# DeltaNet mixer on one Trainium2 core: read-out normed and projected by token block, one weight split moved, one barrier replaced by flags

## The reference, cut to what matters

```python
q, k, v = jnp.split(silu(conv(proj[..., :3*kd])), 3, axis=-1)   # l2norm on q and k
o = gated_delta_rule_chunked(q, k, v, beta, g)                  # chunks of 64 tokens
o = o * lax.rsqrt(jnp.mean(o * o, axis=-1, keepdims=True) + RMS_EPS) * norm_g
o = o * jax.nn.silu(z).reshape(b, s, DN_HEADS, DN_HEAD_DIM)
return h + o.reshape(b, s, kd) @ w_out
```

## Time and profile before

| what | value |
|---|---|
| median of 3 runs | 2733.64 us (2732.69 to 2733.97) |
| the profiled execution | 2735.75 us |
| its span, first to last instruction | 2733.7 us |
| TensorE busy | 2642.7 us, 97% of the span |
| VectorE, ScalarE, GpSimd busy | 2015.5, 1472.7, 86.8 us |
| mean granted TensorE clock | 0.988 of full |

### The profile page before, as it was taken

One profiled execution on the slowest core, in us unless ns is written; L12 is line 12 of the kernel. 1 busy time (PEld: TensorE's weight loads), 2 busy tenths in 40 slices (PEclk: granted clock), 3 DMA queues, 4 the chain that ended last, 5 costly groups with the idle time before them and its releaser, 6 DMA issues.

```text
span 2733.7 us, 46442 instructions
## 1 busy us (share of the span) xinstructions
PE 2642.7 (97%) x18206; PEld 2254.9 (82%) x18206; DVE 2015.5 (74%) x1904; ACT 1472.7 (54%) x1446; POOL 86.8 (3%) x82
## 2 busy tenths in 40 slices
PE   8999999999999989999999898999999999999998
PEld 7889887888889888888889887787787878787776
DVE  6666876666666956676667755888888888888787
ACT  5443514444444514455446624676777677776765
POOL 6000006000000000000000000000000000000000
PEclk9999999999999999999999998999999999999999
DMA  8564313555563305555564405999999999999893
GB/s 275 192 191 154 114 49 124 191 192 171 195 193 129 109 18 170 193 187 170 194 189 139 140 3 200 348 342 348 340 337 349 345 339 347 346 340 346 317 351 119
DMA packets 342896, 601.48 MB, mean 220 GB/s; under 512 B 11984, under 2 KB 180816, under 8 KB 342608
## 3 DMA queue, kind: packets, MB, share of 16 engines
q1 hardware_dynamic: 335264, 590.85, 62.6%
q10 hardware_dynamic: 7472, 8.32, 0.9%
HBM read 598.08 MB, written 1.05 MB: 219 GB/s over the span
## 4 chain that ended last, share of the span: by engine, by line
PE 62%; DMA 22%; DVE 8%; ACT 3%; DVEq 2%; issue 1%; another core or an unknown queue 1%; ACTq 0%; PEldq 0%; SPq 0%; PEld 0%; POOLq 0%
PE ps L2856 13%; PE ps L565 8%; DMA raw<-in_ffn_w_down 8%; PE ps L589 7%; PE ps L2885 7%; PE ps L2860 6%; DMA raw<-in_w_in 6%; PE ps L568 4%; DVE wlo L314 4%; DMA raw<-in_dn_w_in 4%; PE ps L2890 3%; DMA work<-in_moe_w_gate 2%; ACT whi L310 2%; DVEq L316 1%; DMA raw<-in_ffn_w_up 1%
## 5 line engine op out<-in xcount | busy, mean ns | idle before, releaser
L314 DVE TENSOR_TENSOR wlo<-raw,whi 128x2048 fp32r<-128x2048 f32 (+1 forms) x394 | 903.2, 2292 | 217.5 <-ACT whi L310 209.2
L310 ACT CAST whi<-raw 128x2048 fp32r<-128x2048 f32 (+1 forms) x394 | 751.3, 1908 | 402.0 <-DMA raw<-in_ffn_w_down 142.7
L2856 PE MATMUL ps<-whi,xboth 128*128 128x512 f32 x1792 | 459.4, 398 | 6.1 <-issue 2.3
L565 PE MATMUL ps<-xboth,whi 128*128 128x512 f32 x1680 | 420.8, 392 | 0.0
L2856 PEld LDWEIGHTS ps<-whi,xboth 128*128 128x128 f32 x1792 | 330.1, 188 | 81.7 <-issue 15.2
L565 PEld LDWEIGHTS ps<-xboth,whi 128*128 128x128 f32 x1680 | 305.3, 189 | 57.2
L314 DVE TENSOR_TENSOR wlo<-U,whi 128x2048 fp32r<-128x2048 f32 x112 | 256.4, 2289 | 53.4 <-ACT whi L310 50.5
L310 ACT CAST whi<-U 128x2048 fp32r<-128x2048 f32 x112 | 214.2, 1912 | 82.2 <-DMA U<-in_moe_w_up 73.7
L568 PEld LDWEIGHTS ps<-xboth,wlo 128*128 128x128 f32 x1680 | 229.2, 190 | 16.4
L2860 PE MATMUL ps<-wlo,xboth 128*128 128x512 f32 x896 | 240.1, 390 | 0.5 <-DVE wlo L314 0.5
L568 PE MATMUL ps<-xboth,wlo 128*128 128x256 f32 x1680 | 234.2, 282 | 0.0
(11 more groups left out here) (538 smaller groups left out, 3624.7 us busy)
## 6 DMA issues: line engine op xcount, KB each, us to landing
raw<-in_moe_w_gate SPq DMA_DIRECT2D x58, 1024.0 KB, 5.8
raw<-in_moe_w_up SPq DMA_DIRECT2D x56, 1024.0 KB, 6.0
U<-in_moe_w_up SPq DMA_DIRECT2D x56, 1024.0 KB, 5.8
U<-in_moe_w_down SPq DMA_DIRECT2D x56, 1024.0 KB, 5.6
raw<-in_ffn_w_gate SPq DMA_DIRECT2D x55, 1024.0 KB, 5.2
raw<-in_ffn_w_up SPq DMA_DIRECT2D x55, 1024.0 KB, 5.3
raw<-in_ffn_w_down SPq DMA_DIRECT2D x55, 1024.0 KB, 4.8
work<-in_moe_w_gate SPq DMA_DIRECT2D x54, 1024.0 KB, 6.0
```

Of the source, the lines that this page charges most:

```text
L310: act.copy(whi[:, n % SPLIT, 0:width], buf[:, 0:width]).then_inc(hi_ready[n % RAW], 1)
L314: dve.tensor_tensor(wlo[:, n % SPLIT, 0:width], buf[:, 0:width], whi[:, n % SPLIT, 0:width], ALU.subtract).then_inc(split_ready[n % SPLIT], 1)
L565: pe.matmul(ps[:, first_bank + b, :], whi[:, n % SPLIT, c * GW + b * P:c * GW + (b + 1) * P], xboth[:, c].rearrange("p a t -> p (a t)"), s ...
L2856: pe.matmul(dst, part[:, k * C // 2 + c, xhalf(q)], whi[:, (m + k) % SPLIT, c * EW:(c + 1) * EW], start=(k == 0 and c == 0 and part is xhi ...
```

## The change

The last step of dn_in no longer splits a tile; dn_core begins with that split on ScalarE and VectorE. dn_core is taken out of `APART`. TensorE transposes block 0 of the read-out (`dn_turn_out_tensor`) between the two halves of block 1's read-out, and block 1 after the first two weight tiles of the projection. ScalarE and VectorE carry out norm, gate and the split into `xhi` and `xlo` for block 0 and then for block 1, with a flag per part (`dn_lo`) for TensorE. The normed read-out lies in the place of `dn_qe`, since `work[:, 0:2048]` still holds `dn_R`. The projection (`dn_project_tensor`) runs tiles 0 to 2 for block 0, tiles 0 to 2 for block 1, then tile 3 for both; a tile's slot is given back after block 1. ScalarE issues a square root of a constant ahead of its Squares. ScalarE's and VectorE's parts of dn_out stay as they are.

```diff
@@ -171,13 +171,13 @@
-APART = ("rwkv", "dn_in", "dn_core")
+APART = ("rwkv", "dn_in")
@@ -2064,7 +2064,7 @@
 ...
         dn_decayed = state_in(work[:, 9216:10240])
-        dn_sq, dn_on = dn_W, th_in(work[:, 0:2048])
+        dn_sq, dn_on = dn_W, dn_qe
         dn_out = work[:, 2048:4096].rearrange("p (h t) -> p h t", h=NH)
@@ -2249,7 +2249,8 @@
 ...
                 tap.then_inc(f["dn_tap"], 1)
-                split_hi(act, m + SPLIT)
+                if j < DN_TILES - 1:
+                    split_hi(act, m + SPLIT)
                 if 1 <= j <= DN_CONV:
@@ -2324,8 +2325,9 @@
 ...
                     tap.then_inc(f["dn_conv"], 1)
-                take(dve, hi_ready[(m + SPLIT) % RAW])
-                split_lo(dve, m + SPLIT)
+                if j < DN_TILES - 1:
+                    take(dve, hi_ready[(m + SPLIT) % RAW])
+                    split_lo(dve, m + SPLIT)
             return n + DN_TILES
@@ -2337,7 +2339,7 @@
 ...
-        def dn_core_tensor(pe):
+        def dn_core_tensor(pe, n, l):
             for t in range(TT):
@@ -2381,9 +2383,6 @@
 ...
             r0, r1 = HALVES
-            def quarter(first, h):
-                return ps[:, first + h // 4, (h % 4) * P:(h % 4 + 1) * P]
@@ -2436,12 +2435,54 @@
 ...
             dn_out_tensor(pe, 1, 2)
-            for t in range(TT):
-                pe.wait_ge(f["dn_on"], t + 1)
-                for h in range(NH):
-                    tr = pe.transpose(ps[:, (6, 0)[t] + h // 4, (h % 4) * P:(h % 4 + 1) * P], dn_on[:, t, h, :],
-                                      const("ident"))
-                tr.then_inc(f["dn_oT"], 1)
+            return n
+        def dn_turn_out_tensor(pe, t):
+            pe.wait_ge(f["dn_on"], t + 1)
+            if t:
+                pe.wait_ge(f["dn_om2"], 2 * t)
+            for h in range(NH):
+                tr = pe.transpose(quarter(6, h), dn_on[:, t, h, :], const("ident"))
+            tr.then_inc(f["dn_oT"], 1)
+        DN_OUT_TILES = C // 2
+        EARLY_TILES = DN_OUT_TILES - 1
+        def dn_project_part(pe, n, j, t):
+            pe.wait_ge(f["dn_lo"], 2 * t + j // 2 + 1)
+            last = j == DN_OUT_TILES - 1
+            blocks = [(b, s) for b in range(2) for s in range(2)]
+            if last:
+                blocks = [(b, s) for s in range(2) for b in range(2)]
+            for b, s in blocks:
+                for k, (wp, part) in enumerate(PASSES):
+                    mm = pe.matmul(ps[:, 2 * t + s, :], (xhi, xlo)[part][:, 2 * j + b, t * P:(t + 1) * P],
+                                   wp[:, (n + j) % SPLIT, b * D + s * HALF:b * D + (s + 1) * HALF],
+                                   start=(j == 0 and b == 0 and k == 0), stop=(last and b == 1 and k == 2),
+                                   skip_group_check=True)
+                if last and b == 1:
+                    mm.then_inc(f["y_part"], 1)
+            if t == TT - 1:
+                mm.then_inc(tile_done[(n + j) % SPLIT], 1) if not last else pe.drain().then_inc(tile_done[(n + j) % SPLIT], 1)
+        def dn_project_tensor(pe, n, l):
+            for j in range(EARLY_TILES):
+                take_split(pe, n + j)
+                dn_project_part(pe, n, j, 0)
+                if j == 1:
+                    dn_turn_out_tensor(pe, 1)
+            for j in range(EARLY_TILES):
+                dn_project_part(pe, n, j, 1)
+            take_split(pe, n + EARLY_TILES)
+            for t in range(TT):
+                dn_project_part(pe, n, EARLY_TILES, t)
+            return n + DN_OUT_TILES
+        def quarter(first, h):
+            return ps[:, first + h // 4, (h % 4) * P:(h % 4 + 1) * P]
@@ -2456,6 +2497,7 @@
 ...
             if t == 1:
+                dn_turn_out_tensor(pe, 0)
                 pe.wait_ge(f["dn_ss"], 3)
@@ -2466,7 +2508,9 @@
 ...
-        def dn_core_scalar(act):
+        def dn_core_scalar(act, n, l):
+            split_hi(act, n - 1 + SPLIT)
@@ -2490,20 +2534,22 @@
 ...
                 act.copy(dn_A[:, c - 1], wide_two((6, 0)[c - 1])).then_inc(f["dn_as"], 1)
+            act.activation(tiny[:, 72:73], small("one"), ACT.Sqrt)
             for t in range(TT):
 ...
                 act.activation(dn_sq[:, t], wide_two((4, 2)[t]), ACT.Square).then_inc(f["dn_sqd"], 1)
-            act.wait_ge(f["dn_om"], 2)
-            act.activation(dn_ms, dn_tmp, ACT.Sqrt, bias=small("eps"), scale=1.0 / P).then_inc(f["dn_or"], 1)
-            for t in range(TT):
+                act.wait_ge(f["dn_om"], t + 1)
+                act.activation(dn_ms[:, t], dn_tmp[:, t], ACT.Sqrt, bias=small("eps"), scale=1.0 / P).then_inc(f["dn_or"], 1)
                 for q in range(2):
 ...
                              dn_out[:, 4 * q:4 * q + 4, t * P:(t + 1) * P]).then_inc(f["dn_hi"], 1)
-        def dn_core_vector(dve):
+            return n
+        def dn_core_vector(dve, n, l):
             d_ = dve.drain
+            take(dve, hi_ready[(n - 1 + SPLIT) % RAW])
+            split_lo(dve, n - 1 + SPLIT)
             for t in range(TT):
@@ -2537,35 +2583,40 @@
 ...
                     dve.tensor_copy(dn_R[:, 2], bank(2)).then_inc(f["dn_rs"], 1)
+                    dn_unit_vector(dve, 0)
                 d_()
 ...
                 dve.tensor_tensor(dn_S[c], dn_decayed, wide_two((6, 0)[c - 1]), ALU.add).then_inc(f["dn_ss"], 1)
-            for t in range(TT):
-                dve.wait_ge(f["dn_sqd"], t + 1)
-                dve.tensor_reduce(dn_tmp[:, t], dn_sq[:, t], AX.X, ALU.add)
-                d_()
-                dve.tensor_tensor(dn_tmp[:, t], dn_tmp[:, t], dn_rqq[:, t], ALU.mult).then_inc(f["dn_om"], 1)
-            dve.wait_ge(f["dn_or"], 1)
-            dve.reciprocal(dn_ms, dn_ms)
+            dn_parts_vector(dve, 0)
+            dn_unit_vector(dve, 1)
+            dn_parts_vector(dve, 1)
+            return n
+        def dn_unit_vector(dve, t):
+            d_ = dve.drain
+            dve.wait_ge(f["dn_sqd"], t + 1)
+            dve.tensor_reduce(dn_tmp[:, t], dn_sq[:, t], AX.X, ALU.add)
             d_()
-            dve.tensor_tensor(dn_ms, dn_ms, dn_rq, ALU.mult)
+            dve.tensor_tensor(dn_tmp[:, t], dn_tmp[:, t], dn_rqq[:, t], ALU.mult).then_inc(f["dn_om"], 1)
+            dve.wait_ge(f["dn_or"], t + 1)
+            dve.reciprocal(dn_ms[:, t], dn_ms[:, t])
             d_()
-            for t in range(TT):
-                dve.tensor_tensor(dn_on[:, t], wide_two((4, 2)[t]), per_token(dn_ms, t), ALU.mult).then_inc(f["dn_on"], 1)
-            for t in range(TT):
-                dve.wait_ge(f["dn_oT"], t + 1)
-                tk = slice(t * P, (t + 1) * P)
-                for q in range(2):
-                    dve.scalar_tensor_tensor(out=dn_out[:, 4 * q:4 * q + 4, tk], in0=wide_one((6, 0)[t] + q),
-                                             scalar=second_vec("dn_norm_g_2")(0),
-                                             in1=U[:, DN_Z + 4 * q:DN_Z + 4 * q + 4, tk], op0=ALU.mult,
-                                             op1=ALU.mult).then_inc(f["dn_om2"], 1)
-            for t in range(TT):
-                tk = slice(t * P, (t + 1) * P)
-                for q in range(2):
-                    dve.wait_ge(f["dn_hi"], 2 * t + q + 1)
-                    dve.tensor_tensor(xlo[:, 4 * q:4 * q + 4, tk], dn_out[:, 4 * q:4 * q + 4, tk],
-                                      xhi[:, 4 * q:4 * q + 4, tk], ALU.subtract)
+            dve.tensor_tensor(dn_ms[:, t], dn_ms[:, t], dn_rq[:, t], ALU.mult)
+            d_()
+            dve.tensor_tensor(dn_on[:, t], wide_two((4, 2)[t]), per_token(dn_ms, t), ALU.mult).then_inc(f["dn_on"], 1)
+        def dn_parts_vector(dve, t):
+            tk = slice(t * P, (t + 1) * P)
+            dve.wait_ge(f["dn_oT"], t + 1)
+            for q in range(2):
+                dve.scalar_tensor_tensor(out=dn_out[:, 4 * q:4 * q + 4, tk], in0=wide_one(6 + q),
+                                         scalar=second_vec("dn_norm_g_2")(0),
+                                         in1=U[:, DN_Z + 4 * q:DN_Z + 4 * q + 4, tk], op0=ALU.mult,
+                                         op1=ALU.mult).then_inc(f["dn_om2"], 1)
+            for q in range(2):
+                dve.wait_ge(f["dn_hi"], 2 * t + q + 1)
+                dve.tensor_tensor(xlo[:, 4 * q:4 * q + 4, tk], dn_out[:, 4 * q:4 * q + 4, tk],
+                                  xhi[:, 4 * q:4 * q + 4, tk], ALU.subtract).then_inc(f["dn_lo"], 1)
@@ -3239,22 +3290,13 @@
 ...
+        STREAM["dn_core"] = lambda sp, n, l: n
+        TENSOR["dn_core"], VECTOR["dn_core"], SCALAR["dn_core"] = dn_core_tensor, dn_core_vector, dn_core_scalar
+        TENSOR["dn_out"] = dn_project_tensor
```

(15 more changed lines are left out.)

## The result

Four runs of the changed kernel took 2713.44 to 2716.94 us, median **2715.79**; four of the kernel before 2732.69 to 2736.09, median 2733.80. The ratio is 0.9932 [0.9920, 0.9943]: 18.0 us less. The forecast was 2717.2, 16.4 less, in a range of 2714 to 2723. The profiled execution took 2713.44 us, its span is 2711.5, against 2735.75 and 2733.7. It is the fastest of its four, so the two profiles lie further apart than the medians.

The account below looks back on a forecast made before the run. TensorE, with 62% of the span in the chain of waits, was taken to bound the kernel. The moved split's -3.4 and the tail's -13.0 make -16.4 us: 2717.2 on the median 2733.64, range 2714 to 2723.

Parts of the forecast that it names:

- The tail, -13.0: From the read-out's old end to the last projection matmul, TensorE takes 24.1 us in place of 37.1.
- The slacks: In the projection, inputs ready before TensorE asks: 0.9 us at second transposes, 0.3 at block 1's tiles, 0.5 at fourth tile.
- rival (a): In the projection, the new waits come late and become holes, with the clock possibly falling: 2721 us; chance 0.10.
- The moved table load: ScalarE's 1.28 us load for the square root, moved ahead of block 0's Square into an idle stretch: worth nothing.
- The moved split, -3.4: At dn_core's start, TensorE begins earlier and VectorE's second product starts at 1556.88 in place of 1560.25: 3.4 us less.
- everything in the solve follows: In dn_core, all of the solve was to shift with VectorE's second product, by 3.4 us (3.2 with the low clock).
- -4.0, if TensorE alone led: The split term's upper bound in dn_core: 4.0 us less if TensorE, not VectorE, led.
- Rival (b): The moved split sits on dn_core's path, so the first term is 0: 2720.6 us; chance 0.06.
- Route and experts unchanged: The stages behind the projection follow unchanged, so the -13.0 us is kept and the first expert tile comes 16 us earlier.
- (c): The weight copies pace the experts, so that stage starts only 11.0 us earlier: 2722.6 us; chance 0.03.
- (d): Slower than before: copies' lead over the first expert tile shrinks by 5.4 us, experts lose 30 us: 2747; chance 0.03.
- Code placement a microsecond either way: For the total, where the code falls was to spread the forecast by a microsecond either way.

Follow-up runs that it names:

- e3: Changed kernel with the barrier, the old projection by weight tile and the last split in dn_in kept, so only the norm goes by block: 2736.90 us.
- e5: Changed kernel with the projection in the old order, weight tile by weight tile for both token blocks, block 1's transposes ahead of it: 2723.22 us.
- e6: Kernel before with 15 dummy matmuls behind dn_in's last matmul, ahead of the barrier, and TensorE's wait for VectorE's decays ahead of them: 2731.14 us.
- e1: Kernel before with only the last weight split moved from dn_in to the start of dn_core; barriers, norm and projection as they were: 2731.48 us.
- e2: Kernel before with 20 and 17 dummy matmuls on zeros (the fillers) in TensorE's two holes at the end of dn_core: 2740.62 us.
- e8: Changed kernel with 37 tiny matmuls on zeros, without use, in TensorE's hole in the route stage: 2723.04 us.
- e9: Changed kernel with 15 dummy matmuls in the route stage and VectorE's two memsets moved to where it waits for the ranks: 2715.39 us.
- e11: Kernel before, unchanged, profiled once more: 2733.91 us.

## Why the prediction was right

*The tail, -13.0*: measured -13.2; the run that has the tail without the moved split has the same piece, and gains 13.9 us with the route's 1.7 in it. Its parts held too. The first hole is 0.33 us (forecast 0.5); the matmuls took 5.76 + 16.34 = 22.1 (21.8); the two batches of transposes 1.02 and 0.87 (0.9 each). The slacks were enough: block 1 was scaled at 1629.98, 1.2 us before TensorE turned it (0.9); its first subtraction ended at 1634.36, 12 matmuls of 0.227 behind 1632.19 make 1634.91, 0.55 to spare (0.3); the fourth tile's split ended at 1642.19, and 48 matmuls make 1643.1, 0.9 to spare (0.5). The profile confirms the forecast that no wait takes the holes' place, so rival (a) fell. How much of the 13 was the clock: the fillers alone brought 3.4; the other 10 are work of VectorE and ScalarE that now lies beside matmuls. By steps the piece went from 38.71 to 36.44 with the norm by block (e3), to 31.33 with flags in place of the barrier (e5), and to 25.54 with the order by block: 2.3, 5.1 and 5.8 us. The three hold only in this order, each on top of the last. The moved table load adds nothing that shows: before, it was over at 1634.05, and the square root waited for VectorE until 1634.28.

*The moved split, -3.4*: this term was mis-sized, it measured -4.3. TensorE's hole came as forecast (2.70), and the clock stayed at 1.00 in the Gram blocks. The failed step is "everything in the solve follows" VectorE's second product. Counted from dn_in's last matmul, that product moved from 11.16 to 7.98 us (1553.27 + 0.6; -3.2), TensorE's first transposes from 11.05 to 6.63 (-4.4), and the read-out by 4.3: what leads is TensorE's transposes, which ScalarE evacuates (L2519), and the next batch of transposes waits for ScalarE (1561.46, 1.41 us). In the kernel before, both stood 0.11 us apart, so its rows couldn't tell them apart; the bound, "-4.0, if TensorE alone led", was nearer. The -4.3 is 3.2 of hole and 1.05 from the first Gram matmul to the read-out (73.65 in place of 74.70); e6, which has that clock and not the earlier start, gives 1.2 for the second. Rival (b) would have left this term at 0; e1 has 3.3 us for it.

*Route and experts unchanged*: the experts yes (+0.1; SyncE still waits 892.3 us for slots, against 906.3), so rivals (c) and (d) fell. The route no: it was 1.7 us shorter, which the prediction put at nothing. The second router block is 1.93 us in place of 3.56, since the clock fell behind it and not as it began. Why it fell later isn't shown. Before, then after:

```profile
1672.02 2.02 PE L2644 MATMUL ps<-nar,rope 128*128 128x8 f32 x16 [0.41 <-ACT rope L2673]
1673.89 3.56 PE L2644 MATMUL ps<-nar,work 128*128 128x8 f32 x16
...
1683.50 5.68 PE L2909 MATMUL ps<-work 128*128 128x128 f32 x32 [1.36 <-DVEq L2756]
```

```profile
1651.38 1.95 PE L2695 MATMUL ps<-nar,rope 128*128 128x8 f32 x16 [0.41 <-ACT rope L2724]
1653.18 1.93 PE L2695 MATMUL ps<-nar,work 128*128 128x8 f32 x16
...
1661.16 6.17 PE L2960 MATMUL ps<-work 128*128 128x128 f32 x32 [1.36 <-DVEq L2807]
```

*"Code placement a microsecond either way"* was too small for this kernel: 37 instructions at the wrong place cost 7 to 8 us (e2, e8). The change was spared that, with one TensorE row fewer ahead of the loop; the prediction doesn't look at where the code falls, so this is luck.

*Luck in the total*: the split's term was worked out from a profile that has 80.62 us to the read-out, which four of five profiles of that code don't have (83.19 to 83.57). Between those and the changed kernel's 76.35 lie 6.9 us; between 80.62 and the 79.25 that code like its own also has (e1, e9), only 1.4. Which lengths the timed runs had isn't on record; the two of the changed kernel with a mean clock of 0.992 took 2713.44 and 2715.18 us, the two with 0.990 took 2716.40 and 2716.94. The range had nothing for such falls of the clock, and one run of four, 2713.44, lies below it.

## What to carry to other kernels

When a norm or gate stands between two stages of matmuls, look whether it can be done block by block, with the first block's matmuls in the second block's gap. Here that order brought the last 5.8 of 13.2 us, and the norm by block and the missing barrier alone would have stopped at 7.4. Before an edit adds instructions ahead of a long loop, fix the sum with a range for where the code falls: a profile's holes without a releaser, behind each branch back, show it. And where two engines' rows stand a tenth of a microsecond apart, take both moves as the term's two ends.

## What the runs showed of the hardware

**The clock behind a short hole is not the same each time.** Of seven profiles with the split moved, TensorE idle for 2.68 to 2.70 us each, five have 76.33 to 76.35 us to the read-out and two (e1, e9) 79.25 and 79.27. In e9 the clock falls within the Gram blocks and once more in the solve:

```profile
1550.00:1552.00 2.00, 2.00 (x42) 2.00 (x42) 1.60 (x1) 0.26 (x1) 0.00 (x0) 0.50 0.90 347
...
1564.00:1566.00 2.00, 2.00 (x42) 2.00 (x41) 0.18 (x1) 2.00 (x8) 0.00 (x0) 0.50 0.00 0
```

Of five with the split in dn_in (idle 5.9 us), one has 80.62 (the first profile) and four 83.19 to 83.57. There the clock is low in the Gram blocks every time, and in the four again behind the solve's next short hole, as in e11:

```profile
1564.00:1566.00 2.00, 0.00 (x0) 0.00 (x0) 1.85 (x4) 2.00 (x8) 0.00 (x0) 1.00 0.00 0
1566.00:1568.00 2.00, 1.89 (x14) 1.56 (x16) 0.00 (x0) 0.25 (x2) 0.00 (x0) 0.62 0.00 0
```

So the move is worth 80.62 - 76.34 = 4.3 us where the clock doesn't fall in the solve of either kernel, and 83.2 - 79.25 = 4.0 where it falls in both. The longer piece is longer by 2.6 us with the split in dn_in and by 2.9 with it moved; the 2.9 hold a fall in the Gram blocks as well. What decides it in one execution stays open; five of seven against one of five hints that an earlier start also makes it rarer, and is too few to show it.

**A clock that falls while TensorE works.** In the kernel before, TensorE's idle time in the route ahead of the fall is 0.41 us. It is busy all through the two windows below, with the router's products of 8 columns, and the clock falls as the second block of them begins (1673.89), which took 3.56 us:

```profile
1672.42:1673.42 1.00, 1.00 (x11) 1.00 (x10) 0.04 (x1) 0.79 (x4) 0.00 (x0) 1.00 1.01 379
1673.42:1674.42 1.00, 1.00 (x8) 1.00 (x8) 0.38 (x2) 0.33 (x3) 0.00 (x0) 0.67 1.06 391
```

In the changed kernel the same 16 products took 1.93 us. There the clock is 1.00 over 1648 to 1655 and 0.57 on average over the next 6 us, when TensorE stands idle behind them (2.39 us, for VectorE).
